# First x tile and first two weight blocks loaded in halves by two queues; second four blocks rounded ahead of x's second tile

## What is computed

```python
xn = rms_norm(x, g_pre)                       # (320, 2048)
u_a, v_a, z_a, q_b, k_b, v_b, z_b, a_lr, m_a, m_b = split_cols(xn @ w_in)
...                                           # spatial gating branch, gated linear attention branch
m = sigmoid(m_a) * (y_a @ w_pa) + sigmoid(m_b) * (y_b @ w_pb)
h = x + rms_norm(m @ w_o, g_post)
h = h + sigmoid(h @ w_pg) * (p @ w_pe)
```

## Time and profile before

| | |
|---|---|
| median of 3 runs | 951.6 us (951.38 to 951.88) |
| the profiled execution's own time | 951.07 us |
| its span in the records | 949.4 us |
| TensorE busy in the span | 944.8 us (100%) |
| DVE, ACT, POOL busy | 569.7, 377.2, 121.9 us |
| DMA | 159.73 MB, mean 168 GB/s |
| first data matmul starts | 4.69 us |

### The profile page before, as it was taken

The page is one execution under the profiler, slowest core; times in us unless marked ns, Lnnn a source line. Parts: engine busy times, 40 slices in busy tenths (PEclk is TensorE's granted clock), DMA queues, the critical chain, the costliest instruction groups (busy, mean ns, idle before and its releaser), DMA issues.

```text
span 949.4 us, 17453 instructions
## 1 busy us (share of the span) xinstructions
PE 944.8 (100%) x6678; PEld 938.2 (99%) x6678; DVE 569.7 (60%) x800; ACT 377.2 (40%) x485; POOL 121.9 (13%) x113
## 2 busy tenths in 40 slices
PE   9999999999999999999999999999999999999998
PEld 9999999999999999999999999999999999999998
DVE  7948779747889866444454444444545444597442
ACT  7545244522353444333333333333333223555331
POOL 1000005504213730000000000000002333100000
PEclk9999999999999999999999999999999999999999
DMA  9535445978645544444444444444447444347541
GB/s 352 183 127 186 146 129 187 238 251 258 217 156 166 176 147 156 145 155 155 139 148 155 141 152 149 155 149 142 151 158 268 143 153 155 112 133 228 175 159 36
DMA packets 56674, 159.73 MB, mean 168 GB/s; under 512 B 6452, under 2 KB 20280, under 8 KB 56632
## 3 DMA queue, kind: packets, MB, share of 16 engines
q1 hardware_dynamic: 42496, 143.05, 45.5%
q10 hardware_dynamic: 14136, 16.10, 5.1%
HBM read 149.94 MB, written 9.18 MB: 168 GB/s over the span
## 4 chain that ended last, share of the span: by engine, by line
PE 100%; DVE 0%; issue 0%; POOL 0%; DVEq 0%; POOLq 0%
PE bank L1395 30%; PE bank L1396 30%; PE bank L1397 30%; PE bank L1460 1%; PE bank L1661 1%; PE bank L1463 1%; PE bank L1658 1%; PE bank L1664 1%; PE bank L1469 1%; PE bank L1428 0%; PE bank L1427 0%; PE bank L1426 0%; PE bank L1567 0%; PE bank L1433 0%; PE bank L1607 0%; PE bank L1502 0%
## 5 line engine op out<-in xcount | busy, mean ns | idle before, releaser
L744 DVE TENSOR_TENSOR w_lo<-w_raw,w_hi 128x1024 fp32r<-128x1024 f32 x252 | 314.9, 1255 | 317.0 <-ACT w_hi L638 165.9
L1395 PE MATMUL bank<-x_hi,w_hi 128*128 128x320 f32 x1216 | 376.4, 310 | 0.0
L1397 PE MATMUL bank<-x_hi,w_lo 128*128 128x320 f32 x1216 | 375.7, 309 | 0.0
L1396 PE MATMUL bank<-x_lo,w_hi 128*128 128x320 f32 x1216 | 375.7, 309 | 0.0
L417 ACT ACTIVATE w_hi<-w_raw 128x1024 fp32r<-128x1024 f32 x148 | 156.0, 1058 | 251.8 <-PE bank L1397 235.2
L1395 PEld LDWEIGHTS bank<-x_hi,w_hi 128*128 128x128 f32 x1216 | 228.2, 188 | 1.7 <-issue 1.6
L1396 PEld LDWEIGHTS bank<-x_lo,w_hi 128*128 128x128 f32 x1216 | 228.2, 188 | 0.0
L1397 PEld LDWEIGHTS bank<-x_hi,w_lo 128*128 128x128 f32 x1216 | 228.2, 188 | 0.0
L638 ACT ACTIVATE w_hi<-w_raw 128x1024 fp32r<-128x1024 f32 x96 | 101.7, 1059 | 115.6 <-PE bank L1397 115.6
L1395 PE MATMUL bank<-m_hi,w_hi 128*128 128x320 f32 x448 | 138.4, 309 | 0.0
L1396 PE MATMUL bank<-m_lo,w_hi 128*128 128x320 f32 x448 | 138.4, 309 | 0.0
(11 more groups left out here) (253 smaller groups left out, 921.9 us busy)
## 6 DMA issues: line engine op xcount, KB each, us to landing
w_raw<-in_w_units SPq DMA_DIRECT2D x258, 512.0 KB, 3.3
state_dec<-in_s ACTq DMA_DIRECT2D x8, 512.0 KB, 7.4
out_st_dec<-state_dec ACTq DMA_DIRECT2D x8, 512.0 KB, 5.2
h<-in_x_t ACTq DMA_DIRECT2D x4, 640.0 KB, 6.9
out_y<-pe_out ACTq DMA_DIRECT2D x16, 160.0 KB, 2.5
x_sb<-in_x_t SPq DMA_DIRECT2D x6, 320.0 KB, 7.1
v_rows<-v_parts SPq DMA_DIRECT2D x4, 256.0 KB
v_stacked_rows<-v_rows SPq DMA_DIRECT2D x4, 256.0 KB, 7.1
```

The costliest lines, as they stand in the source:

```text
L744: dve.tensor_tensor(wlo[:, q], raw[:, q], whi[:, q].bitcast(F32), ALU.subtract).then_inc(lo_ready, 1)
L1395: pe.matmul(acc, h, hi[:, k0 + k, :], start=first and k == 0, stop=False)
L1396: pe.matmul(acc, h, lo[:, k0 + k, :], start=False, stop=False)
L1397: m = pe.matmul(acc, l, hi[:, k0 + k, :], start=False, stop=last and k == UK - 1)
```

## The change

x's first tile (128 partitions) is loaded as two DMAs of 64 partitions, one by SP and one by ACT, and so are blocks 0 and 1 of unit 0. Blocks 2 and 3 become a DMA of their own on SP's queue, with the new semaphore `w_second`. Who waits for `x_first` and `w_first` now waits for 32. ACT rounds blocks 4 to 7 of unit 0 ahead of x tile 1 instead of behind it. TensorE's matmuls on zeros are seven instead of eight.

```diff
+        w_second = sem("w_second_loaded")
...
-            sp.dma_start(x_0[:, 0:8 + T], A["x_first"]).then_inc(x_first, 16)
+            low, two = slice(0, P // 2), slice(2, WAVE)
+            sp.dma_start(x_0[low, 0:8 + T], A["x_first"][low]).then_inc(x_first, 16)
+            sp.dma_start(raw[low, 0, 0:2], A["w_units"][0][low, 0:2]).then_inc(w_first, 16)
+            sp.dma_start(raw[:, 0, two], A["w_units"][0][:, two]).then_inc(w_second, 16)
...
-            act.dma_start(raw[:, 0, 0:WAVE], A["w_units"][0][:, 0:WAVE]).then_inc(w_first, 16)
+            high = slice(P // 2, P)
+            act.dma_start(x_0[high, 0:8 + T], A["x_first"][high]).then_inc(x_first, 16)
+            act.dma_start(raw[high, 0, 0:2], A["w_units"][0][high, 0:2]).then_inc(w_first, 16)
             act.dma_start(raw[:, 0, WAVE:UK], A["w_units"][0][:, WAVE:UK]).then_inc(raw_loaded[0], 16)
...
                     if k == 1:
+                        act.wait_ge(raw_loaded[0], 16)
+                        act.activation(whi[:, 0, WAVE:UK], raw[:, 0, WAVE:UK], ACT.Copy).then_inc(hi_ready, 1)
                         act.wait_ge(par_loaded, 16)
-                        act.wait_ge(x_first, 16)
+                        act.wait_ge(x_first, 32)
...
                     if k == 0:
-                        act.wait_ge(w_first, 16)
+                        act.wait_ge(w_first, 32)
                         act.activation(whi[:, 0, 0:2], raw[:, 0, 0:2], ACT.Copy).then_inc(hi_first, 1)
+                        act.wait_ge(w_second, 16)
                         act.activation(whi[:, 0, 2:WAVE], raw[:, 0, 2:WAVE], ACT.Copy).then_inc(hi_half, 1)
...
-                    if k in (1, 3):
-                        act.wait_ge(raw_loaded[c], 16)
-                        act.activation(whi[:, c, WAVE:UK], raw[:, c, WAVE:UK], ACT.Copy).then_inc(hi_ready, 1)
+                    if k == 3:
+                        act.wait_ge(raw_loaded[1], 16)
+                        act.activation(whi[:, 1, WAVE:UK], raw[:, 1, WAVE:UK], ACT.Copy).then_inc(hi_ready, 1)
...
-                        dve.wait_ge(x_first, 16)
+                        dve.wait_ge(x_first, 32)
...
-            for n in range(8):
+            for n in range(7):
                 pe.matmul(bank[7][:, 0:P], ak[:, 1, 0, P:SEQ], ak[:, 1, 0, P:SEQ], start=True, stop=True)
```

## The result

The changed kernel takes **953.42 us** (median of 20 runs, 952.57 to 954.09) against 951.55 us (20 runs, 951.16 to 952.74) of the kernel before. The ratio is 1.0019, with a 95% interval of 1.0012 to 1.0025: 1.87 us slower. The forecast was 951.5 us, range 950.6 to 952.6, so it was wrong, and on the side on which it had put little.

The account below looks back on a forecast made before the run. TensorE's work bounds the kernel, with unit 4's landing holding back an earlier start: 951.07 - 0.03 + 0 = 951.04 us for a profiled run, 0.5 more for the median, 951.5 us; range 950.6 to 952.6.

Parts of the forecast that it names:

- The hold at c = 4: At k = 8 TensorE, up to 0.2 us early, waits for unit 4; 0.03 us of the gain is left.
- the later issues of SP: SP's issues move 0.93 us later at no cost; x tile 1 costed at 0, at most 0.3 us.
- The dearer row: Transfers up to unit 4: shorter rows and three more completions cost about 0.1 us, 0.25 at most.
- the row of transfers is dearer: Rival, 22%: unit 4 lands later than 17.76 us and TensorE waits; at 0.25 us dearer, 951.8 us.
- The issues themselves: First loads: a further issue costs about 0.45 us; ACT's table load at 2.2 us, ACT free at 3.69.
- Blocks 2 and 3: SP's third issue lands near 4.3 us, rounded at 4.7; no cost to TensorE, at worst 0.2 us.
- The order on ACT: Blocks 4 to 7 rounded in ACT's idle 0.60 us before x tile 1; `hi_ready` at 5.6 instead of 6.54.
- the seven zeros: Before the first data: two passes less, 0.44 us; TensorE free for data at about 4.22 us.
- The pause ahead of k = 1: TensorE's pause of 0.16 us goes, of which 0.08 is not plain pipelining.
- The clock: At the start TensorE's clock rises at about 4.95 us again, so the 0.38 us gained are worth 0.19.
- the clock rises later: Rival, 8%: seven pairs of zeros and a pause put the rise off; by 3 us it would be 953.1 us.
- The rule on halves: Skill guidance on the start's loads; from its neighbour the forecast took that halves bring nothing but fewer bytes in front.

Follow-up runs that it names:

- b_reorder_alone: Kernel before with only blocks 4 to 7 of unit 0 rounded ahead of x's second tile: 951.65 us, ratio 1.0000.
- a_without_halves: Changed kernel with x's first tile whole on SP and blocks 0 and 1 whole on ACT, the rest kept: 952.16 us, ratio 1.0006.
- a_nine_zeros: Changed kernel with nine matmuls on zeros: 953.11 us, ratio 1.0016.
- a_nine_zeros_alr_late: Changed kernel with nine matmuls on zeros and w_alr (256 KB) loaded behind the constants: 952.74 us, ratio 1.0014.
- b_params_in_three: Kernel before with the parameters loaded in three pieces of columns, two more issues on SP, same bytes: 952.68 us, ratio 1.0012.
- a_eight_zeros: Changed kernel with eight matmuls on zeros: 953.50 us, ratio 1.0019.
- after_look_two: Changed kernel, unedited, run again for a second profile: 953.19 us.
- b_three_zeros: Kernel before with three instead of eight matmuls on zeros: 952.41 us, ratio 1.0011.
- b_reorder_and_alr_late: Kernel before with blocks 4 to 7 rounded ahead of x's second tile and w_alr loaded behind the constants: 951.32 us, ratio 0.9998.
- b_x_in_halves: Kernel before with only x's first tile in halves of partitions on SP's and ACT's queues: 953.99 us, ratio 1.0025.
- b_blocks_two_and_three_on_sp: Kernel before with blocks 2 and 3 of unit 0 as their own DMA, second on SP's queue, no halves: 952.12 us, ratio 1.0006.
- b_params_on_act: Kernel before with the parameters issued third on ACT's queue instead of second on SP's: 952.09 us, ratio 1.0004.

## Why the prediction was wrong, step by step

- **The hold at c = 4 was right**, and it explains most of the numbers: the earliest moment of k = 8 is set by unit 4, an earlier start is given back by then (b_reorder_alone, and most plainly a_without_halves, 0.5 us earlier and 1.5 us later), and in nine of eighteen executions TensorE starts k = 8 within 0.02 us of that moment. But in a late row the units in front of unit 4 hold TensorE too: with unit 4 rounded 0.56 us earlier than in a_nine_zeros (19.14 for 19.70), a_nine_zeros_alr_late was at k = 8 only 0.24 us earlier.
- **The step that failed is the size of the late transfers.** I costed the later issues of SP at nothing (x tile 1 at 0, at most 0.3) because "they are far ahead of their transfers", and read that off unit 4 (issued 8.8, landed 8.9 later), where the row is long full. For the first loads it is not so: x's second tile lands at about 5.35 us in the kernel before, 3.6 us after an issue that has two others in front. In the changed kernel it is issued at 3.17 and lands 3.4 us later, at 6.57, 1.2 us late. There the issue is what the transfer follows. SP reaches the parameters at 2.71 instead of 1.28 us, 1.43 later where I had 0.93, and the row doesn't make that up. An estimate says why: from 2.21 to 3.16 us in the kernel before SP issues an x tile and half a unit, 164 and 262 KB, in 0.95 us, some 450 GB/s, hardly more than the 400 that the engines move when full. The dearer row I put at 0.25 us at most; unit 4 was 1.84 us later between the two profiles, and 1.8 between the middles of the profiles. The rival "the row of transfers is dearer" (22%) had the right consequence, a late unit 4 and a TensorE that waits, with a price seven times too small and another cause: it blamed the form of the transfers, short rows and more completions, where b_params_in_three shows whole loads of the same bytes costing 1.13 us by their issues.
- **The issues themselves.** I took 0.41 to 0.46 us for each, from rows of whole loads. The six loads that are halves, or come next behind one, took 0.58 to 0.85 (SP 0.59, 0.58 and 0.58, ACT 0.60, 0.85 and 0.61 with the load behind). ACT's table load came at 2.98 instead of 2.2, ACT was free at 4.47 instead of 3.69, and the half of blocks 0 and 1 on ACT's queue landed at 4.50 instead of 3.75 (SP's half: 2.3 us after its issue, 3.75). In a_eight_zeros, a_nine_zeros, a_nine_zeros_alr_late and after_look_two it landed at 4.9 to 5.5. x's first tile at 3.48 for 3.5 was right, and worth nothing.
- **Blocks 2 and 3** were ready at 5.8 instead of 4.7, landing 3.3 us after an issue at 2.08; TensorE waited 0.31 us for them.
- **The order on ACT and the seven zeros** cost nothing that can be told from zero, as predicted (951.65 and 951.45). The pause ahead of k = 1 was worth 0.19 us in the kernel before (the loads at 5.87 and 6.65 are 0.78 apart, 0.59 without a pause), not 0.08.
- **The clock.** I forecast a rise at 4.95 again; it was at 8.7. But the profiles show it anywhere from 4.5 to 9.3 us without regard to a pause, and in the second profile of the changed kernel it was up at once and the time no lower (953.19 for 952.96). It can take part when unit 4 is early (b_three_zeros, b_reorder_and_alr_late), and is hidden behind unit 4 when that is late. The rival "the clock rises later" happened in the profile that I saw first, and cost at most 0.18 us there (20.92 less the 20.74 that unit 4 allowed).
- **The range.** The "medians" whose scatter I widened it by (951.07 to 951.88) were times of single executions, not medians.
- **The rule on halves.** The Trainium skill (DMA: Bandwidth & Descriptors, "Rules for kernel authors") has a row on exactly this: two transfers to disjoint halves of the partitions share the same 16 engines either way, and one transfer of 128 partitions is to be used. I weighed its neighbour on issuing engines and drew from it only that the halves bring nothing. The runs agree with the row, b_x_in_halves at 1.0025 (1.0016 to 1.0034), and show a cost where it speaks of no gain; b_x_in_halves has only x's tile in halves, and its weights are whole.

Of the 1.87 us, blocks 2 and 3 as one more load of SP are about 0.55 (b_blocks_two_and_three_on_sp, a_without_halves), and leaving the halves out of the changed kernel wins back about 1.3. The parts don't simply add: x's tile in halves costs 2.4 us in the kernel before. Measured in SP's issue time ahead of the parameters and x's second tile, 0.47 us more gives +0.57 (b_blocks_two_and_three_on_sp), 0.95 gives +1.13 (b_params_in_three), and the change's 1.43 gives +1.87, so 1.2 to 1.3 us for each. But the intervals of the three are -0.2 to 1.4, 0.3 to 2.0 and 1.1 to 2.4 us, and b_x_in_halves and b_params_on_act don't follow this line; that a late row costs is shown, the factor is not. The sums of bytes show two losses that go with two parts of the edit: the halves with the first 5 us, the added loads in front of SP's row with the microseconds from 5 to 11 (269 for 386 GB/s at 7 to 8 us). **Open** is by what mechanism the engines move less in each, what the slower seven runs of b_x_in_halves did, why a load less in front (b_params_on_act) brings unit 4 no sooner, and what sets the moment of the clock's rise.

## What to carry to other kernels

When a stage begins with a row of loads that only just keeps up, price an added load not where it lands but where the compute engine next meets the row: here every load put in front delayed all behind it by about its issue or more, and a half was dearer to issue than the whole. Read how far issues run ahead of transfers at the place in question, not where the row is full. And when a profile shows two losses each as large as the whole, profile the same kernel again before choosing: three profiles of the kernel before differ by 0.9 us in when unit 4 is rounded.

## What the runs showed that I had not expected

- A load of 64 partitions takes 0.58 to 0.60 us to issue on either queue where one of 128 takes 0.41, and the next load on that queue takes 0.57 (SP) and 0.84 (ACT) even when it is whole.
- 256 KB behind a half on ACT's queue landed 4.6 us after its issue, 3.3 us without the half in front.
- 26 KB behind 512 KB on ACT's queue took 4.9 us to land, 3.3 us on SP's queue behind 164 KB.
- TensorE went over to 2.4 GHz anywhere between 4.5 and 9.3 us in executions of nearly the same kernel, while the granted clock read 1.00: in one case it was fast at once behind a pause of 1.32 us, in another slow until about 7.2 us without any pause.
- Halves of partitions went with a third fewer bytes moved in the first 5 us (0.59 to 0.69 MB for 0.93 to 0.99), in every profile.
